# Expert gates of a routed layer as two float32r products instead of one float32 product, with GpSimd making half of the operands

## The reference, cut to what matters

```python
e1 = jnp.take_along_axis(i1, ci // TOPK, axis=-1)
e2 = jnp.take_along_axis(i2, ci % TOPK, axis=-1)
experts = (e1 * N_KEYS + e2).reshape(nc, TOK_CHUNK, PEER_HEADS * TOPK)
gates = jax.nn.softmax(sv, axis=-1)...
hid = jax.nn.gelu(jnp.einsum("td,tkd->tk", xi, u_tab[ei]))
return jnp.einsum("tk,tkd->td", gi * hid, v_tab[ei])
```

## Time and profile before

| | us |
|---|---|
| median of 3 runs (lowest, highest) | 3069.22 (3065.42, 3070.78) |
| the profiled execution: its own time | 3074.24 |
| its span, first to last instruction | 3072.4 |
| TensorE busy with matmuls | 2896.7 (94% of the span) |
| VectorE busy | 1956.4 (64%) |
| ScalarE busy | 1573.0 (51%) |
| GpSimd busy | 23.2 (1%) |

### The profile page before, as it was taken

How to read it: one execution, slowest core, us unless ns; L and a number is a source line. 1 busy time by engine, 2 the same in 40 slices (tenths; PEclk the granted TensorE clock), 3 DMA queues, 4 the chain that set the end, 5 groups by cost and what they waited for, 6 DMA issues and landing times.

```text
span 3072.4 us, 54820 instructions
## 1 busy us (share of the span) xinstructions
PE 2896.7 (94%) x19827; PEld 2656.8 (86%) x19827; DVE 1956.4 (64%) x3147; ACT 1573.0 (51%) x2874; POOL 23.2 (1%) x38
## 2 busy tenths in 40 slices
PE   8989998997899889999999999998899999999998
PEld 7978998996799779999999888877899999978886
DVE  4555554445445775996787555558499778855554
ACT  3434444445544554445776444455444477744444
POOL 0000000001000000000000000000000000000000
PEclk9989999998999999999999999999899999999999
DMA  6415555555355424454444555543345544455554
GB/s 210 158 62 170 187 185 155 182 174 94 110 185 184 134 83 147 163 164 158 139 144 131 184 191 190 190 157 110 117 159 163 167 141 138 144 171 191 190 189 141
DMA packets 131003, 480.14 MB, mean 156 GB/s; under 512 B 14608, under 2 KB 14608, under 8 KB 130480
## 3 DMA queue, kind: packets, MB, share of 16 engines
q1 hardware_dynamic: 126432, 460.38, 45.7%
q0 software_dynamic: 4432, 17.87, 2.4%
HBM read 477.02 MB, written 1.18 MB: 156 GB/s over the span
## 4 chain that ended last, share of the span: by engine, by line
PE 79%; DVE 14%; ACT 5%; issue 1%; DMA 1%; POOL 0%; DVEq 0%; ACTq 0%; SPq 0%; POOLq 0%
PE ps L1447 23%; PE ps L1449 23%; PE ps L1448 23%; DVE wl L779 5%; PE ps L1914 4%; ACT wh L362 2%; PE ps L1548 1%; PE ps L1694 1%; DVE mh L1317 1%; DVE picks L1319 1%; DVE arena L1141 1%; DVE mh L1311 1%; PE ps L1726 1%; PE ps L1880 0%; DMA raw<-stream_dram 0%
## 5 line engine op out<-in xcount | busy, mean ns | idle before, releaser
L779 DVE TENSOR_TENSOR wl<-raw,wh 128x1024 fp32r<-128x1024 f32 x878 | 1075.7, 1225 | 926.9 <-ACT wh L362 921.4
L362 ACT ACTIVATE wh<-raw 128x1024 fp32r<-128x1024 f32 x878 | 930.1, 1059 | 1294.9 <-PE ps L1449 1285.3
L1447 PE MATMUL ps<-xh,wh 128*128 128x256 f32 x4448 | 1291.4, 290 | 42.8 <-DVE wl L779 30.5
L1448 PE MATMUL ps<-xl,wh 128*128 128x256 f32 x4448 | 1262.1, 284 | 0.0
L1449 PE MATMUL ps<-xh,wl 128*128 128x256 f32 x4448 | 1261.3, 284 | 0.0
L1447 PEld LDWEIGHTS ps<-xh,wh 128*128 128x128 f32 x4448 | 856.2, 192 | 65.0 <-issue 38.6
L1448 PEld LDWEIGHTS ps<-xl,wh 128*128 128x128 f32 x4448 | 857.4, 193 | 0.3
L1449 PEld LDWEIGHTS ps<-xh,wl 128*128 128x128 f32 x4448 | 856.2, 192 | 0.0
L1447 PE MATMUL ps<-wh,mh 128*128 128x512 f32 x1264 | 503.4, 398 | 26.2 <-DVE ml L791 13.8
L1449 PE MATMUL ps<-wh,ml 128*128 128x512 f32 x1264 | 500.2, 396 | 0.0
L1448 PE MATMUL ps<-wl,mh 128*128 128x512 f32 x1264 | 499.0, 395 | 0.0
(11 more groups left out here) (275 smaller groups left out, 1870.6 us busy)
## 6 DMA issues: line engine op xcount, KB each, us to landing
raw<-stream_dram SPq DMA_DIRECT2D x878, 512.0 KB, 3.3
arena<-bias_scratch POOLq DMA_DIRECT2D x16, 384.0 KB, 6.6
arena<-norm_rows POOLq DMA_DIRECT2D x4, 1024.0 KB, 6.0
arena<-keys_dram POOLq DMA_DIRECT2D x2, 1024.0 KB, 5.2
arena<-ret_c_dram POOLq DMA_DIRECT2D x1, 1344.0 KB, 5.9
xr<-x_dram POOLq DMA_DIRECT2D x1, 1024.0 KB, 9.3
out_dram<-arena POOLq DMA_DIRECT2D x2, 512.0 KB, 2.9
arena<-rg_w_dram POOLq DMA_DIRECT2D x2, 256.0 KB, 3.0
```

What stands on the lines that cost most here:

```text
L362: A(wh[b % 2][:, :, :], raw[:, b % 4, :].rearrange("p (a b) -> p a b", a=DB), ACT.Copy) \
L779: V.tensor_tensor(wl[b % 2][:, :, :], raw[:, b % 4, :].rearrange("p (a b) -> p a b", a=DB), wh[b % 2][:, :, :].bitcast(F32), ALU.subtract) ...
L1447: M(out_ap, lh, rh, start=first, stop=False, skip_group_check=skip)
L1448: M(out_ap, lh, rl, start=False, stop=False, skip_group_check=skip)
```

## The change

TensorE's four float32 products of a step become eight float32r products: the weighted one-hot of e1 is kept as a high part (ScalarE's copy, now rounded, in `gated`) and a low part (`gated_lo`), each multiplied with the one-hot of e2 and accumulated. The gate itself is split once per layer: ScalarE writes `gT` rounded, VectorE subtracts it from the value in PSUM to get `gT_lo` (two instructions of 128 x 128). GpSimd makes `gated_lo` from `iota`, `e1T` and `gT_lo` in one `tensor_scalar` for each token, four a step, with three buffers; `gates(n)` waits for it as well.

`gated_lo` and `raw_hid` lie where `xr` lies. So GpSimd stores `xr` to memory after issuing the load of the keys, and loads it back when the stage's last products are weighted; `norm(6)` and `norm(8)` wait for that load.

```diff
+                pool.dma_start(x_store.rearrange("(c p) d -> p c d", p=P), xr[:, :, :]).then_inc(x_stored, 16)
+                pool.wait_ge(x_stored, 16 * (k + 1))
+                pool.wait_ge(g_split, k + 1)
+                for n in range(U_STEPS):
+                    if n >= 3:
+                        pool.wait_ge(g_mm, U_STEPS * k + n - 2)
+                    for j in range(4):
+                        t = 4 * n + j
+                        ins = nc.gpsimd.tensor_scalar(gated_lo[:, n % 3, j, :], iota, e1T[:, t:t + 1],
+                                                      gT_lo[:, t:t + 1], ALU.is_equal, ALU.mult)
+                    ins.then_inc(g_gated_lo, 1)
+                pool.wait_ge(g_mul, U_STEPS * (k + 1))
+                pool.wait_ge(g_late, (U_STEPS - 1) * (k + 1))
+                pool.dma_start(xr[:, :, :], x_store.rearrange("(c p) d -> p c d", p=P)).then_inc(x_back, 16)
...
-                    A(pickT[:, 0:3, c * P:(c + 1) * P], ps_x[:, c, 0:384].rearrange("p (a b) -> p a b", a=3),
-                      ACT.Copy).then_inc(p_tc, 1)
+                    A(pickT[:, 0:2, c * P:(c + 1) * P], ps_x[:, c, 0:256].rearrange("p (a b) -> p a b", a=2), ACT.Copy)
+                    A(gT[:, c * P:(c + 1) * P].bitcast(F32R), ps_x[:, c, 256:384], ACT.Copy).then_inc(p_tc, 1)
...
+                        if n == 1:
+                            act.wait_ge(x_stored, 16 * (k + 1))
...
+                    if k in (6, 8):
+                        dve.wait_ge(x_back, 16 * (k // 2 - 2))
...
+                for c in range(NC_T):
+                    t = slice(c * P, (c + 1) * P)
+                    ins = V.tensor_tensor(gT_lo[:, t], ps_x[:, c, 256:384], gT[:, t], ALU.subtract)
+                ins.then_inc(g_split, 1)
...
                     pe.wait_ge(g_gated, U_STEPS * k + n + 1)
+                    pe.wait_ge(g_gated_lo, U_STEPS * k + n + 1)
...
-                        ins = M(ps_a[:, n % 4, j * P:(j + 1) * P], gated[n % 3][:, j, :],
-                                oh[n % 2][:, 4 + j, :].bitcast(F32), start=True, stop=True)
+                        dst = ps_a[:, n % 4, j * P:(j + 1) * P]
+                        M(dst, gated[:, n % 3, j, :], oh[n % 2][:, 4 + j, :], start=True, stop=False)
+                        ins = M(dst, gated_lo[:, n % 3, j, :], oh[n % 2][:, 4 + j, :],
+                                start=False, stop=True)
```

More of the change, by code:

```diff
@@ L100, in build @@
         arena = sb("arena", [32768])
-        xr = sb("xr", [NC_T, D])
+        with nc.sbuf_tensor("xr", [P, NC_T, D], F32) as xr:
+            pass
+        gated_lo = sb("gated_lo", [3, 4, P], F32R)
+        raw_hid = sb("raw_hid", [2, T])
         xh, xl = sb("xh", [DB, T], F32R), sb("xl", [DB, T], F32R)
@@ L109, in build @@
         pickT = sb("pickT", [3, T])
-        picks = sb("picks", [2240])
+        with nc.sbuf_tensor("picks", [P, 2240], F32) as picks:
+            pass
+        gated = sb("gated", [3, 4, P], F32R)
+        gT_lo = sb("gT_lo", [704])[:, 0:T]
         rate = sb("rate", [4])
@@ L198, in build @@
         oh = [t.rearrange("p a (b n) -> p (a b) n", b=2) for t in (mh, ml)]
-        gated = [pick_part(512 * n, 4, P) for n in range(3)]
-        raw_hid = [pick_part(1536 + T * n, T) for n in range(2)]
+        x_store = nc.dram_tensor("residual_rows", (T, D), F32, kind="Internal").ap()
         hid = ar(0, NK, T)
@@ L239, in build @@
         g_mm, g_mul = sem("peer_gates"), sem("peer_weighted")
+        g_split, g_gated_lo = sem("peer_gate_low_parts"), sem("peer_gated_low_rows")
+        x_stored, x_back = sem("residual_stored"), sem("residual_loaded")
         g_put, g_late = sem("peer_gates_put"), sem("peer_late_weighted")
@@ L712, in gate_rows @@
                         t = 4 * n + j
-                        ins = A(gated[n % 3][:, j, :], oh[n % 2][:, j, :].bitcast(F32), ACT.Copy,
+                        ins = A(gated[:, n % 3, j, :], oh[n % 2][:, j, :].bitcast(F32), ACT.Copy,
                                 scale=gT[:, t:t + 1])
@@ L722, in late_hidden @@
                     if n:
+                        if n == 1:
+                            act.wait_ge(x_stored, 16 * (k + 1))
                         if n >= 3:
                             act.wait_ge(g_late, (U_STEPS - 1) * k + n - 2)
-                        A(raw_hid[n % 2][:, 0:known], src[:, 0:known], ACT.Gelu_apprx_tanh)
+                        A(raw_hid[:, n % 2, 0:known], src[:, 0:known], ACT.Gelu_apprx_tanh)
                     A(hid[:, m, known:T], src[:, known:T], ACT.Gelu_apprx_tanh).then_inc(evac, 1)
@@ L1414, in late_weigh @@
                     h = hid[:, U_FREE + n, 0:4 * n]
-                    V.tensor_tensor(h, h, raw_hid[n % 2][:, 0:4 * n], ALU.mult).then_inc(g_late, 1)
+                    V.tensor_tensor(h, h, raw_hid[:, n % 2, 0:4 * n], ALU.mult).then_inc(g_late, 1)
                 onehots(0)
```

## The result

The changed kernel takes 3191.53 us (median of 4 runs, 3187.56 to 3194.79) against 3070.0 us (4 runs, 3065.42 to 3070.91): ratio 1.0411, 95% interval 1.0395 to 1.0427, or +122 us. It is slower, as forecast, but by 4.5 times the forecast 27 us and outside the range.

A forecast was written before the change was run, and what follows sets the result against it. TensorE was taken to bound the gate steps at 3.76 us. Profiled 3074.24 + 25 (GpSimd and VectorE in turns) + 2 (stage starts) = 3101 us, so a median of 3096 us; 8-in-10 range 3040 to 3155 us.

The forecast's parts named there:

- What bounds the kernel: In the two gate stages a step takes what TensorE needs, 3.76 us, of which 0.88 us is the gates' products.
- The products: Eight float32r gate products, bound by weight loads, cost 0.92 us against 0.88: +0.04 us a step, +5 us in all.
- GpSimd's low rows: Four tensor_scalar a gate step at 0.32 us each, 1.28 us; bounds 0.10 and 0.76 us apiece.
- the slow rival: GpSimd's low rows at 0.45 us apiece, in turns with VectorE: +91 + 2 us, 3162 us; chance 0.12.
- The turns: GpSimd alternates with VectorE's two-SBUF-operand instructions in gate steps: 2.68 + 1.28 = 3.96 us a step, +25 us; chance 0.40.
- GpSimd as an engine isn't the bound: In a gate step, even four GpSimd instructions at 0.76 us, 3.0 us, fit into 3.76 us.
- The start of a stage: VectorE's two subtractions and GpSimd's first rows delay each gate stage's start by 1 us, +2 us in all.
- The residual's transfers: Storing xr and loading it back costs nothing; up to +10 us if cover failed; 0.02 for transfers or something unforeseen.

The follow-up runs named there:

- experiments 2: Changed kernel without GpSimd's low rows and with four float32r products a step, high rows only: 3015.34 us, ratio 0.9834 to the kernel before.
- experiment 7: Kernel before with one float32r product per token, high rows only; no split, no residual transfers, nothing on GpSimd: 3008.94 us, ratio 0.9821.
- experiment 1: Changed kernel without GpSimd's low rows; all eight float32r products stay, taking the high rows twice: 3071.64 us, ratio 1.0016 to the kernel before.
- experiment 3: Changed kernel with float32 products of the high rows again; GpSimd still makes low rows but TensorE doesn't wait for them: 3072.8 us, ratio 1.002.
- experiment 4: Complete changed kernel, but VectorE's one-hots read iota from a copy in PSUM instead of SBUF: 3093.69 us, ratio 1.0084 to the kernel before.
- experiment 5: Complete changed kernel, but GpSimd makes a step's four low rows in one 128 x 512 tensor_tensor: 3077.83 us, ratio 1.004 to the kernel before.

## Why the prediction was wrong, point by point

- **What bounds the kernel** was right: the step was TensorE's 3.76 us, and taking four products with their loads from it gave 51 and 56 us (experiments 2 and 7).
- **The products** were right in the mechanism: eight float32r products didn't get cheap, since they stand 0.11 us apart like the float32 ones. Their price was 0.01 us a step, 3.77 against 3.76, where I had 0.04. That I had +5 us for the products and experiment 1 measured +4.9 in all is luck: experiment 3, with float32 products and steps of 3.76 us, measured +6.0. The split of the gate gave 0.4 us of it at each stage's start (TensorE waited 2.50 us there in experiments 1 and 3, against 2.10 and in experiment 7, which has no split); where the rest lies isn't shown. That it is the weight loads that set the distance rests on the earlier trace rows; every run here changed loads and products together. The Trainium skill's 81 ns for a stream of loads and products with 128 columns (TensorE: Matmul & The Clock Gate, Back-to-back issue gap) isn't met: 0.11 us here.
- **GpSimd's low rows: the step that failed.** "I take ScalarE's 0.32": the instruction takes 0.78 us undisturbed, just above the row's upper bound of 0.76 and 2.4 times what I took. The trace had no such instruction, and I priced it by another engine's. At 0.76 us apiece, 4 x 0.76 = 3.0 us would have left only 0.76 us of a step for any wait, and the slow rival, to which I gave 0.12 at 0.45 us apiece, would have been the likeliest.
- **The turns** exist, and the operand in PSUM shows what they hang on (experiment 4). But the sum I made of them, VectorE's 2.68 us plus GpSimd's whole length, was too simple in the other direction: with 0.78 us it gives 5.80 us a step, and 4.71 were measured. An instruction of GpSimd's that is past its first 0.13 us when VectorE starts runs on beside it; only one that starts under VectorE's, or just ahead of it, waits. So of 2.68 us only 4.71 - 4 x 0.78 = 1.59 count. The Trainium skill (SBUF — State Buffer, Who interferes with whom) has the conflict right; that the two exclude each other for an instruction's whole length doesn't hold for GpSimd's `tensor_scalar` here (1549.68 beside 1550.18; it holds VectorE off for 0.3 of its 0.79 us), while experiment 5's `late_weigh` nearly fits it.
- **"GpSimd as an engine isn't the bound"** was wrong with it: it was the bound of every step, with its waits.
- **The start of a stage** was too low: TensorE waited 6.18 us for the first gates, against 2.10 and 2.50 without low rows (experiment 1), because GpSimd's first instruction took 2.66 us under two one-hots in a row. After that idle time the granted clock was 0.50 of full, the 1.2 GHz level, from 1437 to 1441 us. It isn't added to the 122 us: GpSimd was already setting the pace.
- **The residual's transfers** were right as far as the store goes: it was issued at 1173.28 us and landed in 10.9 us, the load in 5.9. TensorE was busy for 6.64 of 7 us from 1173 to 1180 us and for 7.00 of 7 from 1180 to 1187 us. The 0.36 us missing are a wait for `wl` that experiment 7, without the store, has at the same place with the same length.

The start, in TensorE's timeline and the clock:

```profile
1437.19 0.45 PE L1945 MATMUL ps<-mh,gated 128*128 128x128 f32 x1 [6.18 <-issue]
1437.00:1441.00 4.00, 3.81 (x18) 3.84 (x19) 1.32 (x2) 0.38 (x1) 4.00 (x6) 0.50 0.34 121
```

What stays open: what GpSimd's fixed 0.36 us consist of, and why a `tensor_tensor` of 512 columns (1.03 us at least) costs much less than four `tensor_scalar` of 128 (3.12 us). Two operations and two pointers instead of one operation may matter; no run took them apart. A form with one weight load for the high and the low part of a token, adding both into the same columns of PSUM, wasn't tried.

## What to carry to other kernels

An idle engine isn't a free one: before work goes to GpSimd, price its instruction by a run of it, and add VectorE's instructions with two SBUF operands under which it will wait. If it must be there, give it few wide instructions and put an operand of VectorE's into PSUM. And eight float32r products of 128 columns with weights of their own cost what eight float32 halves cost, 0.11 us each here: a cheaper pass gains nothing if the number of weight loads and products stays. Count those.

## What the runs showed of the hardware that was not expected

- GpSimd's `tensor_scalar` of 128 x 128 takes 0.78 us, of 128 x 64 0.57 us.
- Moving one operand of a VectorE instruction to PSUM left that instruction at 1.22 us and cut GpSimd's mean from 1.19 to 1.00 us.
- Who waits depends on who came first and on the instruction: VectorE lost about 0.2 us at most to a `tensor_scalar`, and nothing once that was 0.3 us old, but 0.84 us to a `tensor_tensor` of 512 columns.
